# A two-layer hybrid decoder on one Trainium2 core: weight splits in halves of 128x1024, and a new order of the items

## What is computed

```python
x = x + 0.5 * swiglu(rmsnorm(x, g1), w1, w3, w2)     # feed-forward block 1, inner width 2816
h = rmsnorm(x, g); P = h @ w_in                       # one projection: q, k, v, gates of three branches
ret, swa, mo = retention(...), sliding_window(...), memory_attention(...)
x = x + (sum of sigmoid(gate_b) * (branch_b @ w_up_b)) @ w_o
x = x + 0.5 * swiglu(rmsnorm(x, g2), w1, w3, w2)     # feed-forward block 2, inner width 2816
```

## Time and profile before

| | us |
|---|---|
| median of 3 runs | 1488.12 (1487.14 to 1488.65) |
| the profiled execution | 1486.64 |
| its span, first to last instruction | 1484.7 |
| TensorE busy | 1460.1 |
| VectorE busy | 989.4 |
| ScalarE busy | 873.4 |
| mean granted TensorE clock | 0.996 |

### The profile page before, as it was taken

One profiled execution on the slowest core, in us unless ns is written; L12 is line 12 of the kernel. 1 busy time (PEld: TensorE's weight loads), 2 busy tenths in 40 slices (PEclk: granted clock), 3 DMA queues, 4 the chain that ended last, 5 costly groups with the idle time before them and its releaser, 6 DMA issues.

```text
span 1484.7 us, 17181 instructions
## 1 busy us (share of the span) xinstructions
PE 1460.1 (98%) x6934; PEld 1210.0 (81%) x6934; DVE 989.4 (67%) x874; ACT 873.4 (59%) x1034; POOL 92.8 (6%) x109
## 2 busy tenths in 40 slices
PE   8999999999999999999999999999999999999997
PEld 5887888888888878888788878888888888788886
DVE  6998753663463658888789976545545455688885
ACT  6676655655444437576567665556645444476673
POOL 0000000220000000000000000003200000000000
PEclk9999999999999999999999999999999999999999
DMA  9899755644454546799939887455434644659991
GB/s 371 251 276 248 258 181 175 222 142 142 142 205 184 178 168 266 250 284 295 322 116 288 270 218 282 160 176 206 157 124 161 226 143 170 261 180 287 295 280 42
DMA packets 46493, 319.34 MB, mean 215 GB/s; under 512 B 5232, under 2 KB 5872, under 8 KB 8528
## 3 DMA queue, kind: packets, MB, share of 16 engines
q1 hardware_dynamic: 37392, 259.54, 47.0%
q0 software_dynamic: 6320, 44.96, 15.4%
q10 hardware_dynamic: 2704, 13.76, 2.5%
HBM read 312.99 MB, written 5.24 MB: 214 GB/s over the span
## 4 chain that ended last, share of the span: by engine, by line
PE 92%; DVE 2%; DMA 2%; ACT 2%; issue 1%; SPq 0%; POOLq 0%; POOL 0%; ACTq 0%
PE bank L741 28%; PE bank L743 28%; PE bank L742 27%; PE bank L797 4%; DVE w_lo L1532 1%; PE bank L972 1%; PE bank L1073 1%; PE bank L1055 1%; PE bank L946 1%; DMA raw_b<-in_stream 1%; ACT w_hi L1145 1%; PE bank L958 1%; DMA raw<-in_stream 1%; PE bank L970 0%; SPq L602 0%
## 5 line engine op out<-in xcount | busy, mean ns | idle before, releaser
L1532 DVE TENSOR_TENSOR w_lo<-raw,w_hi 128x2048 fp32r<-128x2048 f32 x179 | 414.0, 2313 | 382.7 <-ACT w_hi L1145 382.5
L1145 ACT ACTIVATE w_hi<-raw 128x2048 fp32r<-128x2048 f32 x179 | 342.4, 1913 | 269.8 <-PE bank L743 257.0
L741 PE MATMUL bank<-w_hi,hT_lo 128*128 128x512 f32 (+1 forms) x876 | 345.0, 394 | 4.2 <-DVE act_a L1596 3.4
L743 PE MATMUL bank<-w_lo,hT_hi 128*128 128x512 f32 (+1 forms) x876 | 338.3, 386 | 0.0
L742 PE MATMUL bank<-w_hi,hT_hi 128*128 128x512 f32 (+1 forms) x876 | 337.7, 385 | 0.0
L741 PEld LDWEIGHTS bank<-w_hi,hT_lo 128*128 128x128 f32 x876 | 164.7, 188 | 41.2 <-issue 5.1
L743 PEld LDWEIGHTS bank<-w_lo,hT_hi 128*128 128x128 f32 x876 | 164.5, 188 | 33.9
L742 PEld LDWEIGHTS bank<-w_hi,hT_hi 128*128 128x128 f32 x876 | 164.8, 188 | 30.9
L741 PE MATMUL bank<-w_hi,bT_lo 128*128 128x512 f32 x320 | 126.1, 394 | 0.0
L743 PE MATMUL bank<-w_lo,bT_hi 128*128 128x512 f32 x320 | 124.7, 390 | 0.0
L742 PE MATMUL bank<-w_hi,bT_hi 128*128 128x512 f32 x320 | 124.6, 389 | 0.0
(11 more groups left out here) (203 smaller groups left out, 2158.8 us busy)
## 6 DMA issues: line engine op xcount, KB each, us to landing
raw<-in_stream SPq DMA_DIRECT2D x177, 1024.0 KB, 4.9
raw_q<-in_stream SPq DMA_DIRECT2D x34, 1024.0 KB, 9.8
raw_b<-in_stream SPq DMA_DIRECT2D x33, 1024.0 KB, 9.3
raw<-in_stream POOLq DMA_DIRECT2D x21, 1024.0 KB, 9.9
raw_b<-in_stream POOLq DMA_DIRECT2D x11, 1024.0 KB, 11.6
raw_q<-in_stream POOLq DMA_DIRECT2D x10, 1024.0 KB, 12.1
raw<-in_stream SPq DMA_DIRECT2D x8, 256.0 KB, 7.3
memT<-in_memt ACTq DMA_DIRECT2D x2, 1024.0 KB, 4.9
```

The lines of the kernel that those rows point to most:

```text
L741: nc.tensor.matmul(dst, xl, wh[:, a:b], start=first, stop=False, skip_group_check=more)
L743: return nc.tensor.matmul(dst, xh, wl[:, a:b], start=False, stop=last, skip_group_check=more)
L1145: nc.scalar.activation(slots(o)[0], raw_slot(s), ACT.Copy).then_inc(hi_split, 1)
L1532: nc.vector.tensor_tensor(lo, raw_slot(s), hi.bitcast(F32), ALU.subtract).then_inc(weights_made, 1)
```

## The change

Each split of a unit is now two instructions of 128x1024 on ScalarE and on VectorE, each with its own signal. TensorE waits for the first half at the head of an item and for the second one where its matmuls come to it. The counters of `weights_made` advance by two per item. The order of the items is now a table per layer and feed-forward block (both layers have the same entries), the mixing part has a new order, and `ADDED` has in block 2 the sum of product 6 of pair 0 made by a transfer, and the one of product 4 of pair 1 by VectorE.

```diff
+PARTS = [slice(0, UW // 2), slice(UW // 2, UW)]
...
-FFN_ORDER = {1: """
-u0.0 u0.1 u1.0 g0 u1.1 d0 g1 p0:5 p0:1 p0:3 p0:6 d1 p0:2 p0:7 p1:5 p0:4 g3 p1:3 p1:1 g2 d3 p1:6 p1:2 p1:7 p2:5 d2 p1:4 g5 p2:3 p2:1 g4 p2:6 d5 p2:2 p2:7 p3:5 d4 p2:4 g7 p3:1 p3:3 p3:6 g6 d7 p3:7 p3:2 p3:4 d6 g9 u10.0 g8 u10.1 d9 d8 g10 mix d10
-""".split(), 2: """
-u0.0 u0.1 u1.0 g0 u1.1 d0 p0:5 p0:1 g1 p0:3 u4.0 p0:6 u4.1 p0:2 p0:7 d1 p0:4 p1:5 g3 p1:1 p1:3 d3 g4 p1:6 g2 p1:2 d4 p1:7 p2:5 p1:4 d2 g6 p2:1 g5 p2:3 p2:6 p2:2 d6 p2:7 p3:5 d5 g8 p2:4 p3:3 p3:1 g7 p3:6 d8 p3:2 p3:7 d7 g10 p3:4 d10 g9 d9
+FFN_ORDER = {(0, 1): """
+u0.0 u0.1 u1.0 g0 u1.1 d0 g1 p0:5 p0:1 p0:3 p0:6 d1 p0:2 p0:7 p1:5 p0:4 g3 p1:3 p1:1 g2 d3 p1:6 p1:2 p1:7 p2:5 d2 g5 p1:4 p2:3 p2:1 g4 p2:6 p2:2 d5 p2:7 p3:5 p2:4 p3:3 g7 p3:1 d4 p3:6 d7 p3:7 g6 p3:2 p3:4 d6 u10.0 g9 u10.1 g8 d9 d8 g10 mix d10
+""".split(), (0, 2): """
+u0.0 u0.1 u1.0 g0 u1.1 d0 p0:5 p0:1 g1 p0:3 p0:6 u4.0 u4.1 p0:7 d1 p0:2 p0:4 p1:5 g4 p1:1 p1:3 g3 d4 p1:6 g2 p1:2 p1:7 p2:5 d3 p1:4 d2 g5 p2:1 g6 p2:3 p2:6 p2:2 d5 p2:7 p3:5 d6 p2:4 g8 p3:3 p3:1 g7 p3:6 p3:2 d8 p3:7 d7 g10 p3:4 d10 g9 d9
...
-ADDED = {(1, 0): (7, 4), (1, 1): (6, 7, 4), (1, 2): (7, 4), (1, 3): (6, 7, 4), (2, 0): (7, 4), (2, 1): (6, 7, 4), (2, 2): (6, 7, 4), (2, 3): (6, 7, 4)}
+ADDED = {(1, 0): (7, 4), (1, 1): (6, 7, 4), (1, 2): (7, 4), (1, 3): (6, 7, 4), (2, 0): (6, 7, 4), (2, 1): (6, 7), (2, 2): (6, 7, 4), (2, 3): (6, 7, 4)}
...
-        def lo_ready(o):
-            return weights_made, lo_at[o]
+        def lo_ready(o, part=1):
+
+            return weights_made, lo_at[o] - 1 + part
...
-                if o >= EARLY:
-                    pe.wait_ge(*lo_ready(o))
                 for t in range(TT):
...
                         if o < EARLY and t == 0:
                             pe.wait_ge(first_lo, o * SUBS + j + 1)
+                        elif t == 0 and j % 2 == 0:
+                            pe.wait_ge(*lo_ready(o, j // 2))
...
             def product(l, f, k, n):
-                pe.wait_ge(*lo_ready(o))
                 for j in range(UB):
+                    if j % 2 == 0:
+                        pe.wait_ge(*lo_ready(o, j // 2))
...
-                nc.scalar.activation(slots(o)[0], raw_slot(s), ACT.Copy).then_inc(hi_split, 1)
+                for part in PARTS:
+                    nc.scalar.activation(slots(o)[0][:, part], raw_slot(s)[:, part], ACT.Copy).then_inc(hi_split, 1)
...
-                dve.wait_ge(hi_split, o - EARLY + 1)
-                nc.vector.tensor_tensor(lo, raw_slot(s), hi.bitcast(F32), ALU.subtract).then_inc(weights_made, 1)
+                for n, part in enumerate(PARTS):
+                    dve.wait_ge(hi_split, 2 * (o - EARLY) + n + 1)
+                    nc.vector.tensor_tensor(lo[:, part], raw_slot(s)[:, part], hi[:, part].bitcast(F32), ALU.subtract)\
+                        .then_inc(weights_made, 1)
```

More of the change, by code:

```diff
@@ L134, in step, with item_of @@
         return {"g": "gt", "d": "down"}[kind], f, int(rest)
[L136 to L148, removed]
+    return [step(t) for t in FFN_ORDER[l, f]]
+ITEMS = [[s for s in ffn_steps(l, 1) + MIX_ITEMS + ffn_steps(l, 2) if s[0] != "gt"] for l in range(DEPTH)]
+NI = len(ITEMS[0])
+AT = [{s: i for i, s in enumerate(items)} for items in ITEMS]
+DOWNS = {(l, f): [s[2] for s in ITEMS[l] if s[:2] == ("down", f)] for l in range(DEPTH) for f in (1, 2)}
+S_STEPS = {(l, f): [ITEMS[l][AT[l]["up", f, 0, 0] + n] for n in S_AFTER[l, f]] for l in range(DEPTH) for f in (1, 2)}
+AFTER_PAIRS = {(l, f): AT[l]["prod", f, len(PAIRS[f]) - 1, 4] for l in range(DEPTH) for f in (1, 2)}
+USED = [[sum(s[0] == "up" and s[3] == 0 or s[0] == "down" and s[2] != DOWNS[l, s[1]][-1]
+             or s[0] == "mix" and not UNITS[s[1]][2] and UNITS[s[1]][0] != "skv" for s in ITEMS[l][:i + 1])
+         for i in range(NI)] for l in range(DEPTH)]
+def item_of(o):
+    return ITEMS[o // NI][o % NI]
 def unit_of(s):
@@ L221, in plan_weights @@
             f, k, m = item[1:]
-            there = lambda p: lo_at[l * NI + AT["prod", f, k, p]]
+            there = lambda p: lo_at[l * NI + AT[l]["prod", f, k, p]]
             parts = []
-            for q in NEEDS.get(m, ()):
-                until = there(LAST_USE[q])
+            for q in needs(l, item[:3], m):
+                until = max(there(p) for p in LAST_USE[q])
                 for p in SUMS:
@@ L245, in plan_weights @@
             held[s] = (until, o)
-    return slot, before, after, lo_at, sum_at, sums_first, loads, raw_of, added_after, added_at
+    return slot, before, after, lo_at, sum_at, sums_first, loads, raw_of, added_after, added_at, sum_behind
 G_FFN1, G_MIX, G_MEM, G_RET, G_FFN2 = (KT * i for i in range(5))
@@ L341, in build @@
 def build(nc, x_in, mem_in, memt_in, stream, gains_in, gfin_in, rot_in, decay_in, mask_in, ident_in, out):
-    banks = plan_banks()
-    where, USES, HIS = banks.at, banks.uses, banks.hi
-    slot_of, slot_before, split_after, lo_at, sum_at, sums_first, loads, raw_of, added_after, added_at = plan_weights()
+    banks = [plan_banks(l) for l in range(DEPTH)]
+    where, USES, HIS = [b.at for b in banks], banks[0].uses, banks[0].hi
+    assert all((b.uses, b.hi) == (USES, HIS) for b in banks)
+    slot_of, slot_before, split_after, lo_at, sum_at, sums_first, loads, raw_of, added_after, added_at, sum_behind = plan_weights()
     ctx = ExitStack()
@@ L510, in used @@
                 return full(l, "up{1}_{2}t1".format(*item))
-            if item[0] == "down" and item[2] == DOWNS[item[1]][-1]:
+            if item[0] == "down" and item[2] == DOWNS[l, item[1]][-1]:
                 return full(l, f"down{item[1]}_11")
@@ L547, in made @@
         def made(l, f, k, n):
-            order = [s[3] for s in ITEMS if s[:3] == ("prod", f, k) and s[3] in half]
+            order = [s[3] for s in ITEMS[l] if s[:3] == ("prod", f, k) and s[3] in half]
             return act_made, pair_no(l, f, k) * 3 + order.index(n) + 1
@@ L783, in wait_out @@
             def wait_out(l, names, then, c=0):
-                last = {where[name][0]: name for name in names}
+                last = {where[0][name][0]: name for name in names}
                 for b, name in last.items():
-                    if b not in {where[t][0] for t in then}:
+                    if b not in {where[0][t][0] for t in then}:
                         pe.wait_ge(*out_of(l, name, c))
@@ L885, in down @@
                         name = f"down{f}_{h}{t}"
+                        if h not in [p[0] for p in parts[:n]]:
+                            pe.wait_ge(*lo_ready(o, h))
                         if first:
```

143 lines of the change are left out of this document (78 added, 65 removed).

## The result

The changed kernel takes 1479.11 us (median of 4 runs, 1478.56 to 1479.32), the kernel before 1487.63 us beside it (1487.06 to 1488.65): a ratio of 0.9944, 95% interval 0.9928 to 0.996. A second time, in a later measurement, it took 1480.04 us against 1487.54 (ratio 0.9949, 0.9937 to 0.9962): 7.5 us. The direction and the largest term were right, the size was not.

The account below looks back on a forecast made before the run. TensorE, busy 98% of the span, was taken as the bound, so only its waits could be won. Terms 3.8 + 1.2 + 0.5 + 0.25 + 0.2 - 0.1 = 5.9 us gave 1488.12 - 5.9 = 1482.2 us, range 1479.5 to 1486.0.

Parts of the forecast that it names:

- The order around product 1 of pair 3, 3.8 us: Block 1, both layers: product 3 of pair 3 placed before it removes TensorE's wait for `act_a`, 2 x 1.88 us.
- The nothing that I took for product 4 of pair 2: Block 1: bank 7 must be free within 2.7 us; loss taken as 0, bounds nothing and 0.9 us each.
- Halves at product 4 of pair 0, 1.2 us: Splits ready 0.8 us earlier remove its waits: 0.9 us in layer 1 and 0.3 us in layer 0.
- The 0.3 us in layer 0: The wait at product 4 of pair 0 in layer 0, claimed to go with halves.
- The start, 0.5 us: Before the first down projection: VectorE's chain ends 0.7 us earlier, part spent at low clock; gain between 0.3 and 0.7.
- The small terms, 0.25 + 0.2 - 0.1: Gains at `hT_lo` between layers (0.25), small block 2 waits and fewer switches (0.2); loss at product 1 of pair 2 (0.1).
- The baseline: Median of three runs of the kernel before, 1488.12 us, from which the 5.9 us were taken.
- The middle of an item, nothing: TensorE's added wait inside each item was priced at 0; as a rival, breaking the stream, 1505 us, chance 0.03.
- The fixed costs: Each added split instruction costs 0.07 us on VectorE and 0.09 us on ScalarE, beside TensorE's work.
- The estimate of 0.19 us for ScalarE: Opposing rule: 0.19 us per added half on ScalarE, shrinking the halves' gains by some 0.3 us in all.
- Banks late again: Rival: product 4 of pair 2 and product 1 of pair 3 wait in both layers; forecast 1485 us, chance 0.15.
- The low clock goes: Rival: TensorE's low clock near the start vanishes or ends earlier, gaining up to 2.4 us: 1479.8 us, chance 0.08.

Follow-up runs that it names:

- the corners: Against the kernel before: only TensorE's waits placed anew, 1486.62 us; that plus halves, 1482.71 us. The change without halves, one wait per item: 1484.27 us.
- the second execution of the change: The changed kernel run again with no edit: 1480.04 us (1478.67 to 1482.45), against 1487.54 us for the kernel before.
- The compared profiles: Profiles of the kernel before and of the changed kernel's first profiled execution: 1486.64 and 1478.56 us.
- the run with one wait: The changed kernel, but TensorE waits at an item's head for both halves of the low part: 1479.10 us, ratio 0.9939 to the kernel before.
- the run of the placed waits: The kernel before with TensorE's wait for the low part placed last ahead of its matmul instead of first: 1486.62 us against 1487.54.

## Why the prediction was wrong, by its own steps

- **The order around product 1 of pair 3, 3.8 us.** Right: 1.75 and 1.79 us of span in the two layers, 3.5 us. The nothing that I took for product 4 of pair 2 rested on the halves, and the corners bear that out: 0.23 and 0.45 us with single splits, none with halves. One thing was not said: halves alone would have given 0.8 us of each of these waits, so the two parts overlap here and their gains don't add.
- **Halves at product 4 of pair 0, 1.2 us.** The step from the halves was right, the one on the transfer failed. The chain from ScalarE's split to the product is 0.7 us shorter with halves, as forecast, and with a transfer of 12 us or less the wait is gone; before, at 11.7 us, it was 0.9 us. But I wrote that the transfer ahead of ScalarE "is itself issued after a low part and comes as much earlier". Its length varies on its own, from 11.2 to 14.2 us, and from 13.2 us on a wait is left: 1.8 us in the second execution of the change. The compared profiles show 1.0 us here, and a median of several runs can hold some of either kind; that the figure came out is in part luck. The 0.3 us in layer 0 is real.
- **The start, 0.5 us.** Failed in its mechanism too. VectorE's low part began 0.7 us earlier (23.44 against 24.11 us), but then VectorE waited for the raw_q of the first sum, and by 29.13 us it had 0.17 us left of it:

```profile
26.92 2.29 DVE L1556 TENSOR_TENSOR raw_q<-raw_q 128x2048 f32<-128x2048 f32 x1 [0.34 <-DMA raw_q<-in_stream]
```

  In the second execution this wait was 1.91 us and the stretch 1.8 us longer. The 0.46 us that the compared profiles show is mostly a shorter low clock (some 0.9 us), less a new wait of 0.52 us for S_lo. Here the figure came out by luck.
- **The small terms, 0.25 + 0.2 - 0.1.** This is the sum's largest error, and the step that failed most: the prediction took the many small losses as nearly untouched, and gave the new places of the waits, which its own diff shows, no term at all. Leaving out the start, product 4 of pair 0 in layer 1 and the two rows of product 1 of pair 3, the span fell by 7.9 - 0.46 - 0.97 - 1.75 - 1.79 = 2.9 us, where I had 0.65 us (0.35, and 0.3 for product 4 of pair 0 in layer 0): 2.3 us too little. Named from the profiles: the places of the waits, which I did not price (0.6 us at eleven waits, run alone); `merged`, 0.1 us a layer, by halves; `hT_lo` between the layers, 0.5 us and not 0.25; product 1 of pair 2, a gain of 0.2 us where I had a loss of 0.1, since its wait is gone; and fewer restarts. A stream that stops, or that comes from transposes, pays 0.08 to 0.11 us at its second matmul; there are nine fewer such in the feed-forward parts now (57, and 66 before), 0.8 us, some of it in the places named above; I had counted two. No run takes these apart one by one.
- **The baseline.** The 1488.12 us of three runs stood 0.5 us above the 1487.63 us beside which the change was timed.
- **The middle of an item, nothing.** Right, by the run with one wait. **The fixed costs** of 0.07 and 0.09 us were right: both low parts together last 2.36 against 2.29 us, both high parts 2.01 against 1.92. The estimate of 0.19 us for ScalarE from the Trainium skill, "VectorE: DVE Perf Modes", section on the TRN2 errata, is not what these rows show.
- **The rivals.** "Banks late again" is real at product 4 of pair 2 without halves, and none in the change. "The low clock goes" was half there: 3.4 us in place of 6.8 in the first profile, 6.8 in the second.

What stays open: why the length of the transfer varies; whether it depends on what the other queue moves at the time was not tested. The runs show that it varies within one program, not why. How often the change meets a long one is not known either: its two profiles have one of each.

## What to carry to other kernels

Run the kernel before and the change twice with a profile, and subtract the times between the same counts of TensorE's matmuls: the stretches that differ between two executions of one program are not the change's. Where a wait's chain leads back to a transfer, price it by the transfer's range from issue to landing, and not by the engine that waits last. Look at the order before adding instructions: exchanging two items of the list gave 3.4 us, as much as the halves (3.4 us on top of the places of the waits) with their 584 instructions more.

## What the runs showed of the hardware that I had not expected

- Two waits ahead of a matmul are not alike. With the one that holds first and the one already met last, the matmul starts 0.05 us after the release in place of 0.14 us, and the second matmul gives 0.03 us of that back.
- An accumulating 1 MB transfer on GpSimd's queue took 12.1 and 14.2 us in two executions of one program, at the same place; over the profiles with the same table of sums there it was 11.2 to 14.2 us.
- The clock near the start was low for 3.4, 6.8 or 10.2 us; the 10.2 us came where TensorE stood still three times, before its matmuls at 34.03, 42.19 and 47.26 us. In the run of the placed waits a wait that lost 2.7 us at 802 us was followed by 1.2 GHz; the 1.8 us lost at 800 us in the second execution of the change was not.
